# Transposes issued ahead of the next scores, scaling one head at a time, and output projections with three open groups and a joint slab of their last k-tiles

## What is computed

```python
# block 1
x = x + moba(rmsnorm(x)) ; x = x + conv_ffn(rmsnorm(x)) ; x = rmsnorm(x)
# moba with 256 tokens and blocks of 256: plain causal softmax attention, 16 heads of 64
qkv = x @ w_qkv ; o = softmax(mask(q k^T / 8)) v ; return o @ w_o
# block 2, every norm shifted and scaled by vectors of c_act @ w_mod
x = x + 0.5 (1 + ga1) * swiglu(h)
x = x + (1 + ga2) * hybrid_mixer(h)      # 8 stick-breaking heads, 8 forgetting (softmax) heads, then @ w_o
x = x + 0.5 (1 + ga3) * swiglu(h)
```

## Time and profile before

| | |
|---|---|
| median of 3 runs | 850.05 us (848.76 to 852.48) |
| the profiled execution's own time | 847.64 us |
| its span | 845.4 us |
| mean granted TensorE clock over the span (1 is 2.4 GHz) | 0.994 |
| PE busy | 808.8 us, 96% |
| DVE busy | 644.1 us, 76% |
| ACT busy | 489.7 us, 58% |

### The profile page before, as it was taken

One profiled execution on the slowest core, in us unless ns is written; L12 is line 12 of the kernel. 1 busy time (PEld: TensorE's weight loads), 2 busy tenths in 40 slices (PEclk: granted clock), 3 DMA queues, 4 the chain that ended last, 5 costly groups with the idle time before them and its releaser, 6 DMA issues. The chain is left out here.

```text
span 845.4 us, 16845 instructions
## 1 busy us (share of the span) xinstructions
PE 808.8 (96%) x6824; PEld 787.5 (93%) x6824; DVE 644.1 (76%) x1331; ACT 489.7 (58%) x1015; POOL 21.0 (2%) x53
## 2 busy tenths in 40 slices
PE   6799998999999999999999999799989999999998
PEld 5798887999999999999999999778878999999998
DVE  5678767998998887999888787867646797665651
ACT  6745545766666655756555556656645675555540
POOL 1000000000000000000000000700000000000000
PEclk9999999999999999999999999999999999999999
DMA  9757463766665997499988886445214678765540
GB/s 297 268 193 233 139 224 125 250 199 200 215 198 175 307 307 267 125 304 337 344 293 287 291 268 214 128 127 186 88 60 144 198 233 290 225 200 181 190 154 26
DMA packets 151069, 179.44 MB, mean 212 GB/s; under 512 B 5712, under 2 KB 141136, under 8 KB 150992
## 3 DMA queue, kind: packets, MB, share of 16 engines
q1 hardware_dynamic: 149536, 177.65, 64.1%
q10 hardware_dynamic: 432, 0.68, 0.2%
q0 software_dynamic: 1024, 0.03, 0.1%
HBM read 177.27 MB, written 1.05 MB: 211 GB/s over the span
## 5 line engine op out<-in xcount | busy, mean ns | idle before, releaser
L914 DVE TENSOR_TENSOR wlo<-raw,whi 128x512 fp32r<-128x512 f32 x528 | 342.7, 683 | 69.1 <-ACT whi L671 68.5
L1291 PE MATMUL bank<-A,whi 128*128 128x256 f32 x1280 | 367.6, 287 | 13.3 <-DVE wlo L914 8.3
L671 ACT ACTIVATE whi<-raw 128x512 fp32r<-128x512 f32 x528 | 308.6, 621 | 107.4 <-PE bank L1293 97.4
L1292 PE MATMUL bank<-A,whi 128*128 128x256 f32 x1280 | 359.8, 281 | 0.0
L1293 PE MATMUL bank<-A,wlo 128*128 128x256 f32 x1280 | 359.7, 281 | 0.0
L1291 PEld LDWEIGHTS bank<-A,whi 128*128 128x128 f32 x1280 | 246.0, 192 | 16.8 <-DVE wlo L914 8.5
L1292 PEld LDWEIGHTS bank<-A,whi 128*128 128x128 f32 x1280 | 244.1, 191 | 1.0 <-issue 1.0
L1293 PEld LDWEIGHTS bank<-A,wlo 128*128 128x128 f32 x1280 | 243.7, 190 | 0.0
L1291 PE MATMUL bank<-Hhi,whi 128*128 128x256 f32 x528 | 146.0, 277 | 0.0
L1293 PE MATMUL bank<-Hhi,wlo 128*128 128x256 f32 x528 | 145.8, 276 | 0.0
L1292 PE MATMUL bank<-Hlo,whi 128*128 128x256 f32 x528 | 145.8, 276 | 0.0
(11 more groups left out here) (148 smaller groups left out, 783.2 us busy)
## 6 DMA issues: line engine op xcount, KB each, us to landing
mring<-in_w_mod SPq DMA_DIRECT2D x72, 512.0 KB, 6.2
raw<-in_ffn_w_up SPq DMA_DIRECT2D x22, 1024.0 KB, 5.1
raw<-in_w_gate SPq DMA_DIRECT2D x22, 1024.0 KB, 5.9
raw<-in_w_up SPq DMA_DIRECT2D x22, 1024.0 KB, 5.9
raw<-in_w_down SPq DMA_DIRECT2D x16, 1024.0 KB, 5.4
raw<-in_w_in SPq DMA_DIRECT2D x12, 1024.0 KB, 5.8
raw<-in_moba_w_qkv SPq DMA_DIRECT2D x11, 1024.0 KB, 6.3
raw<-in_ffn_w_down SPq DMA_DIRECT2D x8, 1024.0 KB, 6.4
```

The costliest lines, as they stand in the source:

```text
L671: act.activation(whi[:, i % SPL, k0:k1, 0:width], raw[:, i % RAW, k0:k1, 0:width], ACT.Copy).then_inc(s_whi, 1)
L914: dve.tensor_tensor(lo, raw[:, i % RAW, k0:k1, 0:width], hi.bitcast(F32), ALU.subtract).then_inc(s_wlo, 1)
L1291: pe.matmul(o, hi, xh, start=kg == 0 and not (j and halved(g)), stop=False)
L1292: pe.matmul(o, hi, xl, start=False, stop=False)
```

## The change

It moves, splits and regroups steps; the matrix products are the same.

- `o_slabs`: three groups are open over k-tiles 0 to 5; one slab "ot" holds k-tiles 6 and 7 of all three (768 columns, DMA rows of 3,072 bytes); group 3 follows whole. Five slabs in place of six per projection. Group 2 accumulates in bank 4 (`S_BANKS[0]`) once the Exp of head 12 has read it. Groups 0, 1 and 2 are evicted after k-tiles 3 and 5 of "ot"; group 3 waits for group 1's eviction.
- `attend`: the pairs in flight advance first, the entering pair's scores come after. A pair always enters 3 rounds after the last.
- "scale" and "stsum" are per head: the first head's at age 2, the second's at age 3, behind the first head's "turn" or "later".
- Forgetting heads are unlocked 3 rounds after their K slab, not 2.
- Start: no squares between the first splits; they come behind the first pieces of slab 1. Slab 2 is not split ahead of the first matmul. "norm" comes at k-tile 4 of slab 1; "gq" and "ccol" after k-tile 5 of slab 1; `cond` is loaded by SP behind slab 2.
- The slab numbers of the modulation steps are shifted to fit.

```diff
     def o_slabs(w):
-        cut = []
-        for lo_k, hi_k in ((0, 6), (6, 8)):
-            for c0 in (0, C):
...
-        return cut + slabs_of("o", w, KD, range(0, D, C))[2:]
+        low = [("o", c0, 0, 6, False, C, w[0:6 * P, c0:c0 + C].rearrange("(k p) c -> p k c", p=P)) for c0 in (0, C, 2 * C)]
+        high = w[6 * P:8 * P, 0:3 * C].rearrange("(k p) c -> p k c", p=P)
+        return low + [("ot", 0, 6, 6, True, C, high)] + slabs_of("o", w, KD, [3 * C])
...
             if n % 2:
                 fill(1, force=True)
                 lower()
-                st.put("sq", "qkv1", n // 2)
         offer(1)
+        for q in (0, 2):
+            fill(1, force=True)
+            lower()
+            st.put("sq", "qkv1", q)
+            st.put("sq", "qkv1", q + 1)
         fill_through(1)
         offer(2)
-        fill_through(2)
-        st.put("gq")
...
             if age == 0:
                 st.put("scores", n)
-            elif age == 2:
-                st.put("stsum" if kind == "sb" else "scale", n)
-            elif age in (3, 4):
+            if age in (3, 4):
                 m = n + age - 3
                 st.put("later" if kind == "sb" else "turn", m)
                 self.w_of[m] = len(self.w_of) + 1
-            elif age == LAST_AGE:
+            if age in (2, 3):
+                st.put("stsum" if kind == "sb" else "scale", n + age - 2)
+            if age == LAST_AGE:
...
-            old = list(flight)
-            if waiting and (not flight or flight[-1][1] > (1 if len(self.heads) % 16 > 12 else 2)):
+            for pair in flight:
+                advance(*pair)
+            if waiting and (not flight or flight[-1][1] > 2):
                 enter()
-            for pair in old:
-                advance(*pair)
             turns[0] += 1
...
-                if deferred and kt == 2:
+                if deferred and kt == (4 if ph == "qkv1" else 2):
...
-                if i == 2 and kt == 6:
+                if i == 1 and kt == 5:
+                    st.put("gq")
                     st.put("ccol")
...
+                while tag == "ot" and kt % 2 == 1 and group - o_group <= kt - 3:
+                    self.group_end[group] = done
+                    self.groups.append((ph, "o", (group - o_group) * C))
+                    evict(group)
+                    group += 1
...
             if tag == "qkv":
-                pending.append(("unlock", ph, c0, turns[0] + 2))
+                pending.append(("unlock", ph, c0, turns[0] + (3 if ph == "qkv3" and c0 >= 2048 else 2)))
...
+            if groups[g][1] == "o" and groups[g][2] == 2 * C:
+                return banks[S_BANKS[0]][:, i * S + c0:i * S + c1]
...
+            sp.dma_start(cact[:, :], a["cond"]).then_inc(s_cond, 16)
...
-            act.dma_start(cact[:, :], a["cond"]).then_inc(s_cond, 16)
...
+                final = last and kt == nk - 1
+                if tag == "ot":
+                    g, kg, final = g - 2 + kt % 3, k0 + kt // 3, kt > 2
                 need.wait_ge(s_wlo, nth("lo", i, kt // 2))
                 xh, xl, ncol = here(tag, ph, kg, g)
-                if kg == 0:
+                if kg == 0 and tag == "o" and c0 == 2 * C:
+                    need.wait_ge(s_exp, soft[12 if ph == "o1" else 28])
+                elif kg == 0:
                     emptied(need, g - 2)
```

More of the change, by code:

```diff
@@ L124, in __init__ @@
         self.w_of = {}
+        self.group_end = {}
         self.unnormed = set()
@@ L236, in attend @@
                 advance(*flight.pop(0))
-            old = list(flight)
-            if waiting and (not flight or flight[-1][1] > (1 if len(self.heads) % 16 > 12 else 2)):
+            for pair in flight:
+                advance(*pair)
+            if waiting and (not flight or flight[-1][1] > 2):
                 enter()
-            for pair in old:
-                advance(*pair)
             turns[0] += 1
-            pend(not any(pair[1] in (3, 4) for pair in old))
+            pend(not any(pair[1] in (3, 4) for pair in flight))
         group, o_group, prev = 0, 0, None
@@ L306, in lay @@
             g = o_group + c0 // C if tag == "o" else group
+            if tag == "ot":
+                g = o_group + 2
             self.group_of[i] = g
@@ L314, in lay @@
             for kt in range(nk):
-                kg = k0 + kt
-                while tag == "o" and kg not in o_ready:
+                kg = k0 + (kt // 3 if tag == "ot" else kt)
+                while tag in ("o", "ot") and kg not in o_ready:
                     if not flight and not waiting:
@@ L336, in lay @@
                     st.put("fpart", i - self.first_of[ph])
-                if scaling and kt % 4 == 3 and i > 56:
+                if scaling and kt % 4 == 3 and i > 55:
                     st.put("xscale", scaling.pop(0))
@@ L350, in lay @@
                         mod_step()
+                while tag == "ot" and kt % 2 == 1 and group - o_group <= kt - 3:
[3 more added lines that the diff above has]
+                    group += 1
             offer(i + SPL)
-            if last:
+            if last and tag != "ot":
                 assert g == len(self.groups)
                 self.groups.append((ph, tag, c0))
+                self.group_end[g] = done
                 group += 1
@@ L523, in chunk_of_group @@
         def chunk_of_group(g):
-            i = last_slab[g]
-            return plan.chunk_done[i, slabs[i][4] // 2 - 1]
+            return plan.group_end[g]
         def res_group(ph, n):
@@ L555, in load @@
                     need.wait_ge(s_wlo, nth("lo", i - RAW, q))
-                sp.dma_start(raw[:, i % RAW, 0:nk, 0:width], src).then_inc(s_raw[i % RAW], 16)
+                to = raw[:, i % RAW, 0:nk, 0:width]
+                if slabs[i][1] == "ot":
+                    to = to.rearrange("p (k g) c -> p k (g c)", g=3)
+                sp.dma_start(to, src).then_inc(s_raw[i % RAW], 16)
             def mod_load(u):
@@ L1247, in _ @@
                        "hcol": gates, "gq": first_columns, "mod": mod_dot, "modout": mod_out, "xscale": scale_x, "evict": evict, "fpart": forget,
-                       "scores": peaks, "scale": scales, "stsum": stick_sums, "later": later, "values": values, "qkn": qk_norm}
+                       "scores": peaks, "scale": scale, "stsum": stick_sum, "later": later, "values": values, "qkn": qk_norm}
             for step in st.list:
@@ L1292, in multiply @@
                     pe.matmul(o, hi, xl, start=False, stop=False)
-                    ins = pe.matmul(o, lo, xh, start=False, stop=last and kt == nk - 1 and (j == 1 or not halved(g)))
+                    ins = pe.matmul(o, lo, xh, start=False, stop=final and (j == 1 or not halved(g)))
                 if kt % 2 == 1:
```

18 lines of the change are left out of this document (5 added, 13 removed).

## The result

The kernel after takes 840.02 us (median of 4 runs, 839.49 to 841.07), the kernel before 850.51 in its 4 runs beside them (848.76 to 852.48): a ratio of 0.9878 with a 95% interval of 0.9853 to 0.9902. I had predicted 840.7. The profiled execution of after took 841.07 us, its span 838.8.

The account below looks back on a forecast made before the run. PE, busy 96% of the span, was taken as the bound, so only its waits could be won. Terms summed to -9.3 us from the profiled 847.6, giving 838.3; plus 2.4 for the median, 840.7, with an 8-in-10 range of 836 to 847.

Parts of the forecast that it names:

- a wait for `wlo` at a slab's start: Sign of being wrong: PE waiting for `wlo` or `whi` at slab starts before 110 us.
- the first pair: Attention's first pair in qkv1: waits for scaling and copy fall from 3.3 to 1.6 us, and a 1.7 us clock dip goes.
- the pairs in mid-phase: Heads 4 to 7 and 8 to 11: 0.35 us gained per pair, -0.7 together, with 0.6 returning before V's transposes.
- The start: In qkv1, the earlier norm lets group 0 be evicted before PE needs it: -1.1 us, bounds 0 and -1.1.
- `cond` leaves the way of the first slabs, which moves nothing that PE waits for: At the program's start, moving the load of `cond` was taken to change no PE wait; no term.
- my terms for qkv1: Mid-phase pairs 0.7, first pair's waits 1.7, clock dip near 41 us 1.7, group 0's eviction 1.1: all gains.
- those for qkv3: Forgetting heads: 0.9 us gained at pair 20 to 23, 2.1 from entering a round later, after q and k norm.
- those for o1 and o3: Gains of 2.2 (V's copy before last turns), 1.9 (last pair's values), 0.8 (weight piece); loss of 3.8 (group 3).
- +3.8 for group 3's wait, -1.9 and -0.8 for what it removes: Output projections: group 3 waits 1.0 us in o1, 2.8 in o3; waits for Olo and a weight piece go.
- The clock: Rival, chance 0.25: the dip at 41.6 stays, or o3's 2.8 us wait makes one: 842.4 us, with both 844.1.
- The waits move: Rival, chance 0.17: ACT's queue sets attention rounds, so gains of 0.7, 0.9, 1.7 and the dip come back: 845.7 us.
- Slower: Rival, chance 0.06: qkv1's weights one slab ahead make PE wait at slabs 2 to 11; 855.7 us at 1.5 each.

## Why the prediction was right, point by point

**Waits.** What I had listed to look for came: L1048 (now L1060) 4.0; V's copy no longer ahead of turns 12 and 28; the norm of q and k, Olo and group 0's eviction gone. I had named a wait for `wlo` at a slab's start as a sign of being wrong: there is one, of 0.18 us at slab 1, and none from slab 2 on. DVE's timeline in o3 for group 3's wait:

```profile
637.04 0.88 DVE L1159 SCALAR_TENSOR_TENSOR XT<-bank,hcol,XT 128x256 f32<-128x256 f32 x2 [0.97 <-PE bank L1302]
...
640.16 0.87 DVE L1159 SCALAR_TENSOR_TENSOR XT<-bank,hcol,XT 128x256 f32<-128x256 f32 x2
```

From 637.04 to the end of the second, 641.03, are 4.0 us, as worked out from the earlier trace rows; PE waited 2.8 and in o1 0.9 (I had 2.8 and 1.0). With group 1 ended 1.4 us earlier the wait is 1.4 and not 2.8: the chain sets it.

**Terms that were mis-sized.** Those for the first pair: I left 1.0 us ahead of turn 0 and 0.6 before V's transposes; together 0.56 are left (0.32 + 0.24). The stretch from slab 2 to slab 5 went from 27.94 to 23.53 us, 4.4 less where my terms (1.7 for the waits, 1.7 for the clock) say 3.4. Those for the pairs in mid-phase: I let 0.6 us come back ahead of V's transposes each time, and all three such waits together are 0.7. (My own figures for PE's arrival there, 62.7 + 2 * 1.36 + 1.1, give 66.5 and not 66.75, so they would have made that wait 0.8, further off still.) Slabs 5 to 10 gained 1.4, not 0.7. The start: group 0's eviction wait of 1.1 went, and 0.6 came back ahead of the norm's product, so that half of that term is left. The step "`cond` leaves the way of the first slabs, which moves nothing that PE waits for" was wrong: with `cond` back, the first weight pieces took 7.4 us to land instead of 6.0, and PE was 1.35 us later in slab 1 in that pair of profiles.

**The sum.** Net of pace and half clock the phases of the two profiled executions of the first comparison add up to 819.1 and 810.3 us: 8.8 less, with 0.65 at the start and one fall of the clock fewer (1.7) 11.2, against my 9.3. Of this the slow pace hid 13.9 - 9.3 = 4.6, which gives the 6.6 between the two profiled executions. By phase, in the table above: my terms for qkv1 (0.7, 1.7, 1.7 and 1.1) say 5.2 and it lost 6.7; those for qkv3 (0.9 and 2.1) say 3.0 and it lost 3.1; those for o1 and o3 (2.2, 1.9 and 0.8 less 3.8) say 1.1 and they lost 0.3, or 0.7 net of the pace; for the start I had nothing and it lost 0.65. The medians, which mix the paces on both sides, differ by 10.5. I forecast 840.7 by adding 2.4 for the median of before. Its profiled execution had three fast down phases and its second one only one, so the offset probably stands for the pace, but I didn't know of the pace when I added it. The terms were 1.9 too small, and the medians moved by 10.5, between the two. That the forecast lies within 0.7 of the measured 840.0 is therefore in part luck.

**The sum is not made of separate parts.** Undone one at a time, the start costs 5.7, the attention order 5.3, the output projections 7.6, the forgetting heads' third round 4.0 and `cond`'s place 2.3, together 24.9 of a change worth 10.5. With intervals of 1.3 to 3.2 us each these are rough; the profiled spans, less slow pace and half clock, say about 20 against about 10 (my own arithmetic). The kernel with the new start and attention and the old projections is only 0.37% faster than before. My "+3.8 for group 3's wait, -1.9 and -0.8 for what it removes" priced the new projections at a loss of 1.1, because I compared them with the old attention order, where the last pair enters a round sooner. In the new order, they save the 4.0 us wait and a fall of the clock. Against the old kernel as a whole the sum for o1 and o3 still holds, as the phases above show. The total came out right since the new version has neither; the split between the terms did not. That the old projections cost this much in the new order is shown; that the load's landing time is the root is read from the queues and was not varied.

**Rivals.** *The clock*, 0.25: its place was right in part. The fall at 41.6 went, and that in o3 came in some executions: of the eight profiles with the 2.8 us wait, three. The third fall that I had worked out from the mean clock stands at 144.0 in before, by PE's 3.2 us wait at the start of up1 ("issue"), and in all fourteen profiles. Near 41 us it fell in both executions of before and with ccol late, and in neither of those with the old attention order alone or the old start alone; a 2.4 us wait had none and a 2.5 us wait had one. The 4.0 us wait in qkv3 had one in all fourteen too, 3.4 us long in five and 6.8 in nine. The Trainium skill ("TensorE: Matmul & The Clock Gate", "HAM oscillation — how this bites in real kernels") ties it to idle gaps; the trace agrees for the two longest waits (4.0 and 3.2), and shows that shorter ones (2.8, 2.5) go with a fall in some executions only. *The waits move*, 0.17: only by 0.7; undoing the order brought 6.2 us of waits back and took 0.7 off ahead of V's transposes. *Slower*, 0.06: no wait of that kind in the ten slabs from 2 to 11.

## What to carry to other kernels

Price a part of a schedule against the order it will stand in, not against the old one: a weight load, a late pair and too few open groups each looked harmless, and where they met PE waited 4.0 us. Before a gain of one per cent is read from two profiles, look at a stretch in which nothing changed; here two of them differed by 2.3 us each, and only medians or waits could be compared. A wait at a buffer is often the sum of an in-order queue: ending the producing group 1.4 us earlier shortened it from 2.8 to 1.4.

## What the runs showed of the hardware

At a granted clock of 1.00 the same matmuls run at one of two paces, 0.1134 or 0.118 us apart (88 k-tiles in 60.1 or 62.4 us). A whole down phase keeps one. A lone product of one column ahead of a slab turned the pace over at each of the 222 places that can be told, and ahead of down2 and down4, where one kernel leaves it out, the pace held. Of fourteen profiled executions down1 was slow in four, down2 in seven and down4 in seven, and after and before each had down2 at both. The half clock came in lengths of 3.4 or 6.8 us, and the same wait brought it in one execution and not in another (2.8 us in o3). The runs of one kernel lay up to 9.4 us apart (845.88 to 855.24, 17 runs of the kernel before); in its two profiles the slow pace cost 9.3 and 14.7 us. The first four weight pieces of 256 KB landed in 7.4 us with another 512 KB beside them and in 5.4 to 6.0 without. The table load took 1.28 us and the Silu behind it started 1.30 after it, as in the earlier trace rows: no drain beside a load in this kernel either.
